# Where the three patterns of attention B are weighed and summed in the mixing stage: GpSimd and VectorE, or VectorE alone

## The reference, cut to what matters

```python
def combine_branches(outs, lses):
    wts = jax.nn.softmax(jnp.stack(lses), axis=0)
    return jnp.sum(wts[..., None] * jnp.stack(outs), axis=0)

def mix_output(oa, ob, subln_g, lam_init, norm_b_g, w_out_l, dtype):
    oa = rms_norm(oa, subln_g) * (1.0 - lam_init)
    ob = rms_norm(ob, norm_b_g)
    o = jnp.concatenate([oa..., ob...], axis=-1)
    return jnp.einsum('btm,md->btd', o, w_out_l)
...
m = mix_output(...)
xp = xp + rms_norm(m, norm_mix_post)
h = rms_norm(xp, norm_ffn_pre)        # input of the feed-forward block
```

## Time and profile before

| what | value |
|---|---|
| median of 3 runs | 3539.95 us (3537.38 to 3547.84) |
| the profiled execution, its own time | 3542.82 us |
| its span in the trace | 3541.0 us |
| busy over the span: PE, DVE, ACT, POOL | 92%, 54%, 39%, 15% |
| mixing stage in the trace | 1681 to 1943 us |

### The profile page before, as it was taken

How to read it: one execution, slowest core, us unless ns; L and a number is a source line. 1 busy time by engine, 2 the same in 40 slices (tenths; PEclk the granted TensorE clock), 3 DMA queues, 4 the chain that set the end, 5 groups by cost and what they waited for, 6 DMA issues and landing times. The chain is left out here.

```text
span 3541.0 us, 58434 instructions
## 1 busy us (share of the span) xinstructions
PE 3250.9 (92%) x19347; PEld 3018.8 (85%) x19347; DVE 1910.3 (54%) x4454; ACT 1376.3 (39%) x2979; POOL 516.0 (15%) x397
## 2 busy tenths in 40 slices
PE   6999999799989995887797899999999999999997
PEld 5999999688989994544586899999999999999997
DVE  5222222477768882433796564476366447636754
ACT  5111111388867762332453233333333333333332
POOL 0011010244510002332453000010010001001000
PEclk9999999899999997999899899999999999999999
DMA  4333335547356667997675675476557547645442
GB/s 129 119 97 105 121 104 147 157 75 152 68 132 165 164 181 234 286 328 233 222 243 180 207 232 176 132 230 200 154 181 234 186 128 228 206 148 151 118 116 81
DMA packets 642920, 597.48 MB, mean 169 GB/s; under 512 B 42729, under 2 KB 565442, under 8 KB 637570
## 3 DMA queue, kind: packets, MB, share of 16 engines
q1 hardware_dynamic: 610806, 461.86, 46.2%
q10 hardware_dynamic: 12814, 70.05, 5.8%
q0 software_dynamic: 19104, 63.06, 5.4%
HBM read 492.42 MB, written 169.68 MB: 187 GB/s over the span
## 5 line engine op out<-in xcount | busy, mean ns | idle before, releaser
L2403 DVE TENSOR_TENSOR ff_wl<-ff_wr,ff_wh 128x1024 fp32r<-128x1024 f32 (+2 forms) x380 | 404.1, 1079 | 282.0 <-ACT ff_wh L2335 281.2
L2335 ACT ACTIVATE ff_wh<-ff_wr 128x1024 fp32r<-128x1024 f32 (+2 forms) x380 | 349.2, 938 | 244.2 <-PE ff_d L2263 124.2
L450 PE MATMUL pj_acc<-hT_h,pj_wh 128*128 128x416 f32 x960 | 340.3, 354 | 9.9 <-POOL pj_wl L367 9.9
L450 PE MATMUL pj_acc<-hT_l,pj_wh 128*128 128x416 f32 x960 | 338.1, 352 | 0.0
L2261 PE MATMUL ff_g<-ff_hh,ff_wh 128*128 128x416 f32 x880 | 310.2, 352 | 27.0 <-DMA ff_hh<-scratch_h2T 24.0
L2261 PE MATMUL ff_u<-ff_hh,ff_wh 128*128 128x416 f32 x880 | 310.9, 353 | 15.0 <-DVE ff_wl L2403 15.0
L2261 PE MATMUL ff_d<-ff_ah,ff_wh 128*128 128x416 f32 x880 | 313.4, 356 | 8.8 <-DVE ff_wl L2403 8.8
L2263 PE MATMUL ff_g<-ff_hh,ff_wl 128*128 128x416 f32 x880 | 312.5, 355 | 1.6 <-issue 1.6
L2263 PE MATMUL ff_u<-ff_hh,ff_wl 128*128 128x416 f32 x880 | 311.7, 354 | 0.0
L2263 PE MATMUL ff_d<-ff_ah,ff_wl 128*128 128x416 f32 x880 | 311.6, 354 | 0.0
L2262 PE MATMUL ff_g<-ff_hh,ff_wh 128*128 128x416 f32 x880 | 308.7, 351 | 0.0
(11 more groups left out here) (266 smaller groups left out, 7062.2 us busy)
## 6 DMA issues: line engine op xcount, KB each, us to landing
ff_wr<-in_w_gate SPq DMA_DIRECT2D x110, 512.0 KB, 4.2
ff_wr<-in_w_up SPq DMA_DIRECT2D x110, 512.0 KB, 5.0
bx_kca<-in_cache_a_k SPq DMA_DIRECT2D x128, 256.0 KB, 11.5
sa_vca<-in_cache_a_v POOLq DMA_DIRECT2D x128, 256.0 KB, 7.6
out<-in_cache_win_k ACTq DMA_DIRECT2D x64, 511.0 KB, 4.6
out<-in_cache_win_v ACTq DMA_DIRECT2D x64, 511.0 KB, 4.8
ff_wr<-in_w_down SPq DMA_DIRECT2D x80, 384.0 KB, 4.1
ff_wr<-in_w_down SPq DMA_DIRECT2D x80, 320.0 KB, 3.4
```

The costliest lines, as they stand in the source:

```text
L450: m = pe.matmul(acc[g][:, 0:PG], weights[:, k, c], part[:, c, cols], start=start, stop=stop)
L2335: act.activation(wh[:, slot, 0:size], wr[:, slot, 0:size], ACT.Copy).then_inc(w_hi, 1)
L2403: dve.tensor_tensor(wl[:, slot, 0:size], wr[:, slot, 0:size], wh[:, slot, 0:size].bitcast(F32), ALU.subtract).then_inc(w_lo, 1)
```

## The change

VectorE gets all three multiplications, in the order of patterns 1, 2, 0, then a wait on its own semaphore and the addition of patterns 1 and 2. All this stands in `combine_first`, ahead of `mixed_low`. GpSimd keeps `add_input` alone. `combine_sum` keeps its place and its addition.

```diff
         def _(pool):
-            def combine_rest(m):
-                k = m % 2
-                pool.wait_ge(mix_in[k], raised(mix_loaded(m)))
-                if m == 0:
-                    pool.wait_ge(prep, raised(8))
-                for p in (1, 2):
-                    o = ob[:, k, p].rearrange("p (h e) -> p h e", h=B_HEADS)
-                    last = pool.tensor_tensor(o, o, wg[:, p, m].rearrange("p (h o) -> p h o", o=1)
-                                              .to_broadcast([P, B_HEADS, 64]), ALU.mult)
-                last.then_inc(b_part, 1)
-                pool.wait_ge(b_part, raised(m + 1))
-                pool.tensor_tensor(ob[:, k, 1], ob[:, k, 1], ob[:, k, 2], ALU.add).then_inc(b_rest, 1)
...
             for n in SLOTS_:
-                if 0 <= n + 2 < LAST:
-                    combine_rest(n + 2)
                 if 0 <= n - 1 <= LAST:
                     add_input(n - 1)
...
             def combine_first(m):
                 k = m % 2
                 dve.wait_ge(mix_in[k], raised(mix_loaded(m)))
-                o = ob[:, k, 0].rearrange("p (h e) -> p h e", h=B_HEADS)
-                w = wg[:, 0, m].rearrange("p (h o) -> p h o", o=1)
-                dve.tensor_tensor(o, o, w.to_broadcast([P, B_HEADS, 64]), ALU.mult).then_inc(b_part2, 1)
+                for p in (1, 2, 0):
+                    o = ob[:, k, p].rearrange("p (h e) -> p h e", h=B_HEADS)
+                    w = wg[:, p, m].rearrange("p (h o) -> p h o", o=1)
+                    last = dve.tensor_tensor(o, o, w.to_broadcast([P, B_HEADS, 64]), ALU.mult)
+                last.then_inc(b_part2, 1)
+                dve.wait_ge(b_part2, raised(m + 2))
+                dve.tensor_tensor(ob[:, k, 1], ob[:, k, 1], ob[:, k, 2], ALU.add).then_inc(b_rest, 1)
...
             def combine_sum(m):
                 k = m % 2
-                dve.wait_ge(b_part2, raised(m + 2))
                 dve.wait_ge(b_rest, raised(m + 1))
                 dve.tensor_tensor(cm[:, k, 512:D], ob[:, k, 0], ob[:, k, 1], ALU.add).then_inc(b_sum, 1)
```

More of the change, by code:

```diff
@@ L1672, in mix @@
         h_out = [s.sem(f"h_out{i}") for i in range(2)]
-        (b_part, b_part2, b_rest, b_sum, squared, ss_ok, sd_ok, rs_ok, scaled, gain_ok, turned, high, low, mul, z_sq, z_ss,
+        (b_part2, b_rest, b_sum, squared, ss_ok, sd_ok, rs_ok, scaled, gain_ok, turned, high, low, mul, z_sq, z_ss,
          z_sd, z_rs, z_ok, x1_ok, x_sq, x_sd, x_rs, h_ok, turned2, high2, low2) = (s.sem(n) for n in (
-             "b_part", "b_part2", "b_rest", "b_sum", "squared", "ss_ok", "sd_ok", "rs_ok", "scaled", "gain_ok", "turned",
+             "b_part2", "b_rest", "b_sum", "squared", "ss_ok", "sd_ok", "rs_ok", "scaled", "gain_ok", "turned",
              "high", "low", "mul", "z_sq", "z_ss", "z_sd", "z_rs", "z_ok", "x1_ok", "x_sq", "x_sd", "x_rs", "h_ok",
```

## The result

The changed kernel took 3563.32 us (median of 4 runs, 3558.55 to 3566.13), the kernel before beside it 3541.89 us (median of 4). The ratio is 1.0055, with an interval of 1.0037 to 1.0073: slower, by 13 to 26 us. The forecast was 3554, 3545 to 3561. The direction and the mechanism came as forecast, and the time lies 2 us above the range. Timed again in five rounds, the same program gave 1.0037 (1.0024 to 1.0049): 13.6 us between the medians, where 14 were forecast.

The account below looks back on a forecast made before the run. PE was taken as the bound at 12.86 us per slot, passing to DVE: 9.86 + 1.92 + 2.22 = 14.00. Over slots 1 to 13, less the start's gain, +14.0 us: 3542.8 to 3556.8, less 2.9, 3554; range 3545 to 3561.

Parts of the forecast that it names:

- PE was the bound, DVE had 9.9 us of work and 3 of blocking: Mixing stage before the change: PE sets 12.86 us per slot; DVE needs 9.86 unblocked, POOL's blocking costs it some 3.
- 1.92 us added in a slot: DVE's list: two multiplications and one addition, 1.80 us, plus 0.12 for its own semaphore wait, giving 11.78 per slot.
- The stall of 2.22 us behind the first multiplication, and turns between the engines: POOL's residual gets in after DVE's first multiplication; the second ends at 3.50 us instead of 1.28, making the slot 14.00.
- The row that spoke for the rival: Slot 0: POOL's L1755 lost a turn to DVE's L1913, favouring a hidden stall, slot 12.8 us, total 3539; chance 0.15.
- The start earns 0.9 us before slot 1: Stage start, slots -2 to 0: less waiting for POOL brings slot 1's L1895 from 1727.57 to about 1726.65 us.
- +14.0 us in all: Slots 1 to 13 at 14.00 us: slot 14 begins at 1908.7, where PE transposed tile 15 at 1894.69 before.
- The price of the lost clock: Mixing stage: PE's gaps lower its clock; slots up to 25.7 us, three such slots add 35, total 3589; chance 0.02.
- The Trainium skill's hint that offloading between DVE and GpSimd might not help: DVE and GpSimd share a port; by that, moving the work back would cost nothing either, total 3540 us.
- The rule of the exclusive lock: A DVE operation with two SBUF inputs and a GpSimd operation exclude each other; trace cited: 1.70 us against 0.68.
- rows 8: Profile rows from slot 0, where POOL's L1755, issued at 1717.47, ran only after DVE's L1913, issued at 1718.05.
- the median of the runs shown is 2.9 lower, so I say 3554: Last step, whole kernel: profiled execution of 3542.8 us becomes 3556.8, and the runs' median lies 2.9 us lower.
- the scatter of medians: Whole kernel: allowance widening the forecast from 3552 to 3557 us to 3549 to 3560; that forecast had chance 0.80.

Follow-up runs that it names:

- residual_on_dve: The changed kernel with POOL's residual also on DVE, behind combine_first, POOL idle in the stage: ratio 1.0006 (0.9995 to 1.0017), DVE's slot 12.94 us.
- residual_twice: The changed kernel with POOL computing the residual a second time into a free buffer: no time ratio; slot 16.25 us, mixing stage 308.82 us.

## Why the prediction was right, and where it missed

- *PE was the bound, DVE had 9.9 us of work and 3 of blocking:* right. With POOL idle, DVE's slot in residual_on_dve is 12.94, that is 9.86 + 1.92 + 1.13 (its residual) = 12.91.
- *1.92 us added in a slot:* right; from L1899 to L1908 it is 2.54 us in slots without a residual (1712.37 to 1714.91), where one multiplication had 0.60: 1.94.
- *The stall of 2.22 us behind the first multiplication, and turns between the engines:* right: 4.09 against 1.89 us is 2.20. The row that spoke for the rival did not repeat in any slot with a residual.
- *The start earns 0.9 us before slot 1:* right, 0.98. The L1895 of slot 1 came 46.55 us after the stage's first instruction (1727.57 - 1681.02), and its successor comes at 45.57.
- *+14.0 us in all:* the stage gives +14.4, slot 14 +14.3 where 14.0 was forecast. The sum was 0.4 short; 0.3 of it is the slot's 14.02 for 14.00, 13 times.
- *The price of the lost clock* was read from rows that aren't alike, a pair of matmuls beside the mean of one. Like for like, a pair takes 1.06 us at the stage's start, at a clock of 0.50 (1.2 GHz), and 0.63 in slot 12, and pairs start 0.86 and 0.46 us apart. The factor of 2 was near this 1.9, and the rival didn't come: the clock stays at 1.00.
- *The Trainium skill's hint that offloading between DVE and GpSimd might not help ("Perfetto Trace Analysis", "Optimizing Scalar/DVE Operations")* leaned to no change. By that the ratio would be 1; it is 1.0037 in the five rounds. The rule of the exclusive lock ("SBUF — State Buffer") agrees with the blocked rows: 2.90 us for 0.68 beside the residual, and 1.28 for a pair with an input in PSUM. Why in rows 8 the L1913, issued later than POOL's L1755, went first, isn't shown.
- *The step that failed* is the last: "the median of the runs shown is 2.9 lower, so I say 3554", with 3549 to 3560 for the scatter of medians. The mechanism's terms stood; the term mis-sized was the scatter, of the base and of the changed kernel's own runs. The prediction allowed about 3 us to either side of 3552 to 3557. From 3554 to the measured 3563.3 it is 0.4 us of the stage, 1.9 by which the kernel before itself stood higher beside the changed one (3541.89 for 3539.95), and 7.0 in the median of four runs. The median of the later 12 runs is 4.8 us lower (3558.5). How large such scatter is, the unchanged kernel shows: it ran from 3533.44 to 3554.98 us in the 29 runs of one comparison, its stage before the mixing stage ends anywhere between 1674.7 and 1685.3 us in three traces, and against itself it showed a ratio of 1.0013. An estimate of the range from those 29 runs, some 10 us to either side of the sum, would have reached 3564. The interval given with the result, from 13 us up, did include the 14.

## What to carry to other kernels

Before moving work between VectorE and GpSimd, write down for each of VectorE's instructions where its inputs lie, and lay the two lists side by side. Those with two inputs in SBUF ran one after the other with GpSimd's here; those with an input in PSUM were the cover for GpSimd's, and so were the reductions, with one input in SBUF. The price of a move is the blocking that it creates next to the neighbour's longest instruction; here one wait more was worth 12 us, another order of the same instructions 11, and that order with the residual in halves 15. And before a range is written, look how far the runs of the unchanged kernel are apart, and which stage makes them so.

## What the runs showed of the hardware that was not expected

- With two instructions queued on GpSimd and three on VectorE, the engines took turns one by one (6.29 to 6.34 us for three multiplications beside two residuals, in 13 slots of residual_twice). In the one exception noted, behind L1889, the next instruction of VectorE went first; it was not explained.
- A reduction on VectorE is not blocked: in the kernel before, L1941 (issued at 1747.45) kept its 0.68 us beside GpSimd's two L1755 (1747.03 to 1749.08), which kept 2.05; L1951, issued at 1748.41 beside the same two, took 1.75 us for its 1.28.
- Doing the residual on VectorE costs 1.13 us, on GpSimd 2.38 to 2.40 for the same 128x1024: beside a bound engine the slower engine's length is what is waited for.
- The same program timed against itself in five rounds gave 1.0013 (1.0002 to 1.0025).
